# Gates taken straight from the adaLN sums, and a reordered pooling mixer

## The reference

```python
cond = jax.nn.silu(c)
for layer in range(2):
    mod = (cond @ ada_w[layer] + ada_b[layer]).reshape(B_, N_MOD, D)
    sh1, sc1, g1, sh2, sc2, g2, sh3, sc3, g3 = [mod[:, i] for i in range(N_MOD)]
    h = rmsnorm(x, norm_g[layer, 0]) * (1 + sc1) + sh1
    x = x + 0.5 * g1 * swiglu(h, ff_w13[layer, 0], ff_w2[layer, 0])
    h = rmsnorm(x, norm_g[layer, 1]) * (1 + sc2) + sh2
    mix = even_mixer(h, ...) if layer == 0 else multiscale_pool(h, pool_w[0], pool_b[0], pool_scale[0])
    x = x + g2 * mix
    h = rmsnorm(x, norm_g[layer, 2]) * (1 + sc3) + sh3
    x = x + 0.5 * g3 * swiglu(h, ff_w13[layer, 1], ff_w2[layer, 1])
# multiscale_pool: (((window mean of h) - h) @ w_grp, in 4 groups, + b_grp) * scale
# swiglu: (silu(a) * b) @ w2, with a, b = halves of h @ w13; width 2816
```

## Time and profile before

| | us |
|---|---|
| median of 3 runs (lowest, highest) | 1016.52 (1016.01, 1017.73) |
| the profiled execution, its own time | 1016.09 |
| its span, first to last instruction | 1014.0 |
| busy: TensorE, VectorE, ScalarE, GpSimd | 944.9, 727.4, 433.7, 102.7 |
| mean granted TensorE clock | 0.982 of 2.4 GHz |

### The profile page before, as it was taken

The page is one execution under the profiler, slowest core; times in us unless marked ns, Lnnn a source line. Parts: engine busy times, 40 slices in busy tenths (PEclk is TensorE's granted clock), DMA queues, the critical chain, the costliest instruction groups (busy, mean ns, idle before and its releaser), DMA issues.

```text
span 1014.0 us, 11292 instructions
## 1 busy us (share of the span) xinstructions
PE 944.9 (93%) x4368; PEld 772.7 (76%) x4368; DVE 727.4 (72%) x789; ACT 433.7 (43%) x555; POOL 102.7 (10%) x179
## 2 busy tenths in 40 slices
PE   4799999999889588999999999999999779999998
PEld 4688788887667457888888878888878668888886
DVE  4785978867778856879888677878775677654543
ACT  1444334344446554633333464333343464343431
POOL 2011111101402100011111000111110000000000
PEclk9999999999999789999999999999999979999999
DMA  9989998654994005999999459985894378656221
GB/s 341 376 291 376 377 318 272 228 179 147 327 231 134 34 20 180 351 319 325 349 313 338 170 163 324 298 293 188 290 305 161 103 228 303 206 166 208 83 79 47
DMA packets 147125, 239.34 MB, mean 236 GB/s; under 512 B 16128, under 2 KB 108160, under 8 KB 146944
## 3 DMA queue, kind: packets, MB, share of 16 engines
q1 hardware_dynamic: 126768, 167.01, 50.2%
q0 software_dynamic: 19440, 71.31, 20.1%
q10 hardware_dynamic: 864, 0.30, 0.1%
HBM read 237.54 MB, written 1.05 MB: 235 GB/s over the span
## 4 chain that ended last, share of the span: by engine, by line
PE 77%; DVE 8%; DMA 4%; ACT 4%; issue 3%; SPq 3%; POOL 1%; DVEq 0%; ACTq 0%
PE ps L1364 48%; PE ps L1421 7%; PE ps L1422 7%; PE ps L1425 7%; DMA raw<-in_ff_w 2%; SPq L389 2%; DMA raw<-in_w_in 2%; PE ps L1397 2%; DVE xn L983 1%; PE ps L1436 1%; PE ps L1456 1%; PE ps L1356 1%; DVE x L987 1%; ACT arena L601 1%; ACT hi L577 1%
## 5 line engine op out<-in xcount | busy, mean ns | idle before, releaser
L1364 PE MATMUL ps<-hi,hT_hi 128*128 128x512 f32 (+1 forms) x848 | 339.8, 401 | 13.6 <-DVE lo L874 6.1
L1364 PE MATMUL ps<-hi,hT_lo 128*128 128x512 f32 (+1 forms) x848 | 331.2, 391 | 0.0
L1364 PE MATMUL ps<-lo,hT_hi 128*128 128x512 f32 (+1 forms) x848 | 331.1, 390 | 0.0
L874 DVE TENSOR_TENSOR lo<-raw,hi 128x2048 fp32r<-128x2048 f32 (+1 forms) x76 | 171.6, 2261 | 44.2 <-ACT hi L577 44.1
L1364 PEld LDWEIGHTS ps<-hi,hT_hi 128*128 128x128 f32 x848 | 161.0, 190 | 52.3 <-issue 9.9
L1364 PEld LDWEIGHTS ps<-hi,hT_lo 128*128 128x128 f32 x848 | 160.8, 190 | 33.8
L1364 PEld LDWEIGHTS ps<-lo,hT_hi 128*128 128x128 f32 x848 | 161.2, 190 | 32.7 <-issue 1.4
L577 ACT ACTIVATE hi<-raw 128x2048 fp32r<-128x2048 f32 (+1 forms) x76 | 143.7, 1892 | 41.3 <-DMA raw<-in_ff_w 23.2
L480 POOL DMA_DIRECT2D ada<-in_ada_w x132 | 70.8, 537 | 503.7 <-DVE acc L926 193.4
L926 DVE SCALAR_TENSOR_TENSOR acc<-ada,cond,acc 128x1024 f32<-128x1024 f32 x73 | 93.6, 1282 | 10.5 <-DMA ada<-in_ada_w 6.9
L874 DVE TENSOR_TENSOR lo<-arena,hi 128x2048 fp32r<-128x2048 f32 x30 | 68.7, 2289 | 13.3 <-ACT hi L577 13.3
(11 more groups left out here) (162 smaller groups left out, 1071.9 us busy)
## 6 DMA issues: line engine op xcount, KB each, us to landing
raw<-in_ff_w SPq DMA_DIRECT2D x204, 512.0 KB, 5.6
ada<-in_ada_w POOLq DMA_DIRECT2D x132, 512.0 KB, 6.3
arena<-in_ff_w SPq DMA_DIRECT2D x60, 512.0 KB, 6.2
raw<-in_w_in SPq DMA_DIRECT2D x24, 512.0 KB, 7.6
arena<-in_ada_w SPq DMA_DIRECT2D x4, 1024.0 KB, 18.7
raw<-in_w_out SPq DMA_DIRECT2D x8, 512.0 KB, 4.6
raw<-in_ada_w SPq DMA_DIRECT2D x2, 1024.0 KB, 15.0
arena<-in_b_rpb SPq DMA_DIRECT2D x16, 128.0 KB, 9.9
```

The source lines that it names most:

```text
L874: ins = V.tensor_tensor(lo, src, hi.bitcast(F32), ALU.subtract)
L1364: ins = mm(out, a, b, start=first and m == 0, stop=last and m == len(pairs) - 1, skip_group_check=shared)
```

## The change

- The sum of a gate is not transposed any more. TensorE multiplies the adaLN buffer itself by ones, which sums over the partitions and spreads the result. The bias comes in at the start: ScalarE fills the buffer with eight diagonal blocks, `ident` times the bias column (`gate_start`), and VectorE's first tile adds to them in place of overwriting. The 0.5 is applied by ScalarE's copy.
- A gate is now made in the pair where its vector's sum would have been. `GATE_AT`, `diag`, `diag_buf` and `pool_gate` are gone.
- The vectors are worked on in the order `VECTORS`: 5 after 7, 11 after 13, 14 after 16. So the attention mixer's tiles are those of gate 5, and the last vector of feed-forward 2 is gate 14.
- Gate 14: VectorE multiplies its buffer by `pool_scale` at the end of feed-forward 2; TensorE makes the gate after `pool_average` of tile 0, ScalarE copies it ahead of `norm_out` of tile 1.
- ScalarE's and VectorE's splits of piece 84, and ScalarE's of 85, move into the end of feed-forward 2; VectorE's split of 85 stands ahead of the first difference.
- In the pooling mixer ScalarE takes norm and mean in twos; the biases of two groups are added together; tile 0's residual is done in both parts before tile 1's first, and tile 1's second before `norm_split` of tile 0. The squares follow that order.

The diff, cut to its core; for edits that only rename a wait's count "..." stands.

```diff
-GATE_AT = {(0, 8): 0, (1, 8): 2, (2, 7): 3, (2, 9): 4, (3, 9): 5}
+VECTORS = (0, 1, 2, 3, 4, 6, 7, 5, 8, 9, 10, 12, 13, 11, 15, 16, 14, 17)
...
+def is_gate(g):
+    return VECTORS[g] % 3 == 2
+def gate_of(g):
+    return VECTORS[g] // 3
+def columns_before(g):
+    return sum(not is_gate(i) for i in range(g))
+def acc_before(g):
+    return max(i for i in range(g) if (i in ACC_IN_XN) == (g in ACC_IN_XN))
+def first_pair(g):
+    return next((f, p) for f in range(4) for p in range(PAIRS) if (g, 0) in ada_in_pair(f, p))
...
 # scalar
             def gate_copy(k, half, bank):
                 act.wait_ge(gate_ps, 2 * k + half + 1)
-                dst = pool_gate if k == 4 else gate
-                nc.scalar.activation(dst[:, half * 512:half * 512 + 512], ps[:, bank, :], ACT.Copy).then_inc(gate_ready, 1)
+                nc.scalar.activation(gate[:, half * 512:half * 512 + 512], ps[:, bank, :], ACT.Copy,
+                                     scale=1.0 if k in (1, 4) else 0.5).then_inc(gate_ready, 1)
+            def gate_start(g):
+                before = acc_before(g)
+                if is_gate(before):
+                    act.wait_ge(gate_ps, 2 * gate_of(before) + 2)
+                else:
+                    act.wait_ge(mod_ps, 2 * columns_before(before) + 2)
+                if g == 13:
+                    act.wait_ge(xT_done, 16)
+                for k in range(KT):
+                    nc.scalar.activation(acc_of(g)[:, k * P:(k + 1) * P], ident[:, :], ACT.Copy,
+                                         scale=adab[:, VECTORS[g], k:k + 1]).then_inc(gate_bias, 1)
...
+                    for g in range(2, len(VECTORS)):
+                        if g != 7 and is_gate(g) and first_pair(g) == (f, p + 1):
+                            gate_start(g)
...
                 u_high_tile(f, 1)
+                if f == 2:
+                    split_hi(2 * FFN_PAIR[3])
                 if f < 3:
                     norm_out(s, 0, 4, 8)
+                if f == 2:
+                    split_hi(2 * FFN_PAIR[3] + 1)
...
             ffn(2)
+            for half in range(2):
+                gate_copy(4, half, half)
             g4 = NMOD + 3
-            for half in range(2):
-                norm_out(4, 1, 4 * half, 4 * half + 4)
-                for j in range(4 * half, 4 * half + 4):
+            for j2 in range(0, KT, 2):
+                norm_out(4, 1, j2, j2 + 2)
+                for j in range(j2, j2 + 2):
...
-            split_hi(2 * FFN_PAIR[3])
             norm_squares(5, 0, 0)
+            norm_squares(5, 0, 1)
             norm_squares(5, 1, 0)
-            norm_squares(5, 0, 1)
-            split_hi(2 * FFN_PAIR[3] + 1)
             norm_out(5, 0)
...
 # vector
                 if j == 0:
...
+                    if is_gate(g):
+                        dve.wait_ge(gate_bias, KT * (gate_of(g) + 1))
+                        V.scalar_tensor_tensor(dst, w, cond[:, 0:1], dst, ALU.mult, ALU.add).then_inc(ada_used, 1)
+                    else:
+                        V.tensor_scalar(dst, w, cond[:, 0:1], None, ALU.mult).then_inc(ada_used, 1)
...
                 u_low_tile(f, 1)
                 if f < 2:
                     norm_split(s, 0, ((4, 4),))
+                if f == 2:
+                    dve.wait_ge(pool_in, 32)
+                    dve.wait_ge(ada_used, ada_count(16, KT - 1))
+                    V.tensor_tensor(acc_of(16), acc_of(16), v_sb[:, 1, :], ALU.mult).then_inc(pool_step, 1)
+                    make_acol(5)
+                    split_lo(2 * FFN_PAIR[3])
                 residual(s, 1, y1_half, f + 1, part=0)
...
             ffn(2)
-            dve.wait_ge(pool_in, 32)
-            dve.wait_ge(gate_ready, 10)
-            V.tensor_tensor(gate[:, :], pool_gate, v_sb[:, 1, :], ALU.mult).then_inc(pool_step, 1)
+            split_lo(2 * FFN_PAIR[3] + 1)
...
-            dve.wait_ge(pool_step, 1)
-            make_acol(5)
-            split_lo(2 * FFN_PAIR[3])
-            for t in range(TT):
-                residual(5, t, unit_used, 2 * POOL_PAIR + 1, part=0)
+            residual(5, 0, unit_used, 2 * POOL_PAIR + 1, part=0)
             residual(5, 0, y0_done, 5, part=1)
+            residual(5, 1, unit_used, 2 * POOL_PAIR + 2, part=0)
             norm_scale(5, 0)
-            split_lo(2 * FFN_PAIR[3] + 1)
+            residual(5, 1, unit_used, 2 * POOL_PAIR + 2, part=1)
             norm_split(5, 0)
-            residual(5, 1, unit_used, 2 * POOL_PAIR + 2, part=1)
             norm_scale(5, 1)
...
 # tensor
-            def gate_half(k, half, bank, src=diag_buf):
-                pe.wait_ge(diag_done, KT * (k + 1))
-                mm(ps[:, bank, :], ones[:, :], src[:, half * 512:half * 512 + 512], start=True, stop=True
+            def gate_half(g, half, bank):
+                pe.wait_ge(ada_used, ada_count(g, KT - 1))
+                mm(ps[:, bank, :], ones[:, :], acc_of(g)[:, half * 512:half * 512 + 512], start=True, stop=True
                    ).then_inc(gate_ps, 1)
+            def sum_half(g, half, bank):
+                if half and is_gate(g):
+                    pe.wait_ge(gate_ready, 2 * gate_of(g) + 1)
+                elif half:
+                    pe.wait_ge(mod_red, 2 * columns_before(g) + 1)
+                (gate_half if is_gate(g) else mod_half)(g, half, bank)
+            def sum_read(g):
+                if is_gate(g):
+                    pe.wait_ge(gate_ready, 2 * gate_of(g) + 2)
+                else:
+                    pe.wait_ge(mod_red, 2 * columns_before(g) + 2)
...
+            def pool_bias(t, first=0, last=4):
+                for g in range(first, last):
+                    mm(ps[:, 2 * t + g // 2, (g % 2) * 256:(g % 2) * 256 + 256], ident[:, :],
+                       v_sb[:, 0, g * 256:(g + 1) * 256], start=g % 2 == 0, stop=False, skip_group_check=True)
...
             pool_average(0, 4, 8)
+            pe.wait_ge(h32_done, h32_count(4, 0, KT))
+            pe.wait_ge(pool_step, 1)
+            for half in range(2):
+                gate_half(16, half, half)
...
                 if g % 2 == 0:
                     pe.wait_ge(h32_done, h32_count(4, 1, 2 * g + 4))
-                for t in range(TT):
-                    mm(ps[:, 2 * t + g // 2, (g % 2) * 256:(g % 2) * 256 + 256], ident[:, :],
-                       v_sb[:, 0, g * 256:(g + 1) * 256], start=True, stop=False)
+                    for t in range(TT):
+                        pool_bias(t, g, g + 2)
```

More of the change, by code:

```diff
@@ L306, in build_program @@
         ada_used, mod_ps, mod_red, mod_done = sem("ada_used"), sem("mod_ps"), sem("mod_red"), sem("mod_done")
-        diag_done, gate_ps, gate_ready = sem("diag_done"), sem("gate_ps"), sem("gate_ready")
+        gate_bias, gate_ps, gate_ready = sem("gate_bias"), sem("gate_ps"), sem("gate_ready")
         x_tmp, x_done = sem("x_tmp"), sem("x_done")
@@ L647, in ffn @@
                 for p in range(LAST):
-                    gate_of = GATE_AT.get((f, p))
+                    g = sum_in_pair(f, p)
+                    gated = g is not None and is_gate(g)
                     if p:
@@ L915, in ada_tile @@
                 if j == 0:
-                    if g >= 2:
-                        before = max(h for h in range(g) if (h in ACC_IN_XN) == (g in ACC_IN_XN))
-                        dve.wait_ge(mod_ps, 2 * (before + 1))
-                    if g == 8:
-                        dve.wait_ge(gate_ps, 4)
-                    if g in (1, 9, 13):
-                        dve.wait_ge(xT_done, {1: 4, 9: 12, 13: 16}[g])
-                    V.tensor_scalar(dst, w, cond[:, 0:1], None, ALU.mult).then_inc(ada_used, 1)
+                    if g >= 2 and not is_gate(g):
+                        before = acc_before(g)
+                        if is_gate(before):
+                            dve.wait_ge(gate_ps, 2 * gate_of(before) + 2)
+                        else:
+                            dve.wait_ge(mod_ps, 2 * columns_before(before) + 2)
+                    if g in (1, 9):
+                        dve.wait_ge(xT_done, {1: 4, 9: 12}[g])
+                    if is_gate(g):
[3 more added lines that the diff above has]
+                        V.tensor_scalar(dst, w, cond[:, 0:1], None, ALU.mult).then_inc(ada_used, 1)
                 else:
@@ L1020, in ffn @@
                     tiles, g = ada_in_pair(f, p), sum_in_pair(f, p)
+                    if g is not None and is_gate(g):
+                        g = None
                     if p:
@@ L1464, in ffn @@
                 for p in range(1, LAST):
-                    g, k, spare = sum_in_pair(f, p), GATE_AT.get((f, p)), spare_bank(f, p) + 1
-                    summed = sum_in_pair(f, p - 1)
-                    if summed is not None:
-                        pe.wait_ge(mod_red, 2 * (summed + 1))
-                    if (f, p - 1) in GATE_AT:
-                        pe.wait_ge(gate_ready, 2 * GATE_AT[f, p - 1] + 2)
+                    g, spare = sum_in_pair(f, p), spare_bank(f, p) + 1
```

(13 more changed lines are left out.)

69 lines of the change are left out of this document (24 added, 45 removed).

## The result

| | before | after |
|---|---|---|
| median (lowest to highest), 4 runs each | 1017.12 (1016.01 to 1020.17) | 1007.29 (1002.47 to 1008.45) |
| the profiled execution | 1016.09 | 1008.45 |
| its span | 1014.0 | 1006.5 |

The account below looks back on a forecast made before the run. TensorE, busy 93% of the span, was taken as the bound. Terms 2.90 + 0.88 + 3.04 + 5.4 + 0.88 = 13.1 us off 1016.09 gave 1003.0, as a median 1003.4 us; 8 in 10 range 1000.3 to 1007.6.

Parts of the forecast that it names:

- Transposes of the gates: Six gate vectors no longer transposed; a vector's sum costs TensorE 0.88 us, a gate 1.72 us.
- the 1.72 of pair 8: Feed-forward 0: the gate moves from pair 8 to pair 3, so its 1.72 us at pair 8 go.
- Pair 3 of feed-forward 0: The gate's second half no longer waits for VectorE's reduction, so w2 begins 1.18 us earlier.
- Rival 3: Earlier gate doesn't help feed-forward 0, as the loads holding it up to 91 us return: 2.9 less, 1006.3; chance 0.08.
- Mixer: Attention mixer: 0 gained, bounds 0.53 us lost and 1.6 us gained or lost by the clock.
- Diagonals: Eight ScalarE bias instructions a gate at 0.30 us, 2.4 us (1.7 to 3.8), all hidden: 0; uncovered up to 3.8 us.
- End of feed-forward 2: Gate 11 and two sums replace four sums and two gates: 3.04 us, plus 0.44 counted in the tail; moved splits fit.
- what follows comes 0.44 us earlier (no half-sum): End of feed-forward 2: work after TensorE's w13 comes 0.44 us earlier, VectorE's tile 1 residual due at 789.33, not 789.77.
- Pooling mixer: Between feed-forwards 2 and 3: tile 1 starts at 821.35, not 826.76, at half clock: 5.4 us.
- rival 1: Pooling mixer: clock stays up through the shorter gap, 7.45 us gained there: 1001.4; chance 0.22.
- Rivals 2: Pooling mixer gives nothing, only matmuls count, 7.7 + 0.44: 1008.4; chance 0.12.
- 4 (late loads of 84 and 85): Slower: 84 and 85 landing late delay tile 1's squares and the pooling mixer: 1017 and more; chance 0.04.

Follow-up runs that it names:

- `before_a`: The kernel before, unchanged, run once more for the scatter of its own trace; 1019.56 us.
- `extra`: Changed kernel with four unread transposes put back ahead of every half of a gate, eight per gate vector; 1010.46 us, ratio 0.9911 to the kernel before.
- `swap23`: Changed kernel with vectors 2 and 3 swapped, so the sum is again in pair 3 of feed-forward 0; 1011.03 us, ratio 0.9926 to the kernel before.
- `order_old`: Changed kernel with tile 0's residual in one go undone and ScalarE's squares in their old order, splits left as changed; 1006.52 us.
- `clock_up`: Changed kernel plus 14 and 3 unused 512-column matmuls before and behind the pooling mixer's tile 0 transposes; 1004.68 us, ratio 0.9867 to the kernel before.
- `splits_back`: Changed kernel with only the splits of 84 and 85 back at their old places, residual in one go kept; 1011.08 us, ratio 0.9918 to the kernel before.
- `gates_only`: Changed kernel with the pooling mixer's splits, pooled pieces in fours, residuals' and squares' order put back; grouped biases and gate 14 stay; 1009.38 us.

## Why the prediction was right, and where it was off

The forecast was 1003.4, range 1000.3 to 1007.6; the median came to 1007.29, in the range, 3.9 over the forecast. It was right in sign and, in the main, in mechanism. The sum was too large in the terms that hang on waits, not in those made of matmuls. Between the two traces the gain is 7.5 of the 13.1 us forecast: 2.3 us are missing at the end of feed-forward 2 and in the pooling mixer, and the other 3.3 lie in ff0, the mixer and the first loads, which scatter. So the place inside the range, 0.3 us from its end, owes something to luck, and 7.5 us is itself one draw: the trace of `before_a` and the first of the changed kernel are 11.0 us apart.

- **Transposes of the gates.** The 0.88 of ff1 and ff3 measured 0.90 and 0.88, the 1.72 of pair 8 1.75. `extra` shows the cause.
- **Pair 3 of feed-forward 0, predicted 1.18.** From VectorE's split of the late weights to w2, the chain took 11.71 us before and 10.46 after: 1.25. Two things I had not in the term: the first matmul behind the remaining wait takes 0.27 us longer, and the loads came 0.6 to 1.2 us later, by scatter of their own (`before_a` has it too). Rival 3, "loads return", is what happened in part: ff0 gave 1.50 of 2.90 against the first trace of before (1.25 + 1.75 - 1.21 by the loads - 0.27). Against `before_a` it gave 3.7, for there the sum's wait cost the clock too. One trace of before could not show how far its own scatter reaches.
- **Mixer, predicted 0 with 1.6 us either way by the clock.** +0.84 between the two traces. Its loads scatter by 49.7 to 54.8 us and its rest by 105.3 to 107.0, with both traces of before at the low end. Four changed kernels are there too, at 105.3 to 105.5, so the change doesn't cost a fixed amount; whether it makes a slow rest likelier is open. The multiply-add does what was said: TensorE's wait near 258 us is 1.01 to 1.06 us in every changed kernel, 0.47 and 0.49 before, and it is swallowed by the loads.
- **Diagonals, estimated at 0.30 us each and hidden.** Eight take 2.44 us:

```profile
52.78 2.44 ACT L641 ACTIVATE acc<-ident,adab 128x128 f32<-128x128 f32 x8
```

  The estimate of 2.4 stands; the estimate of 3.2 from the budget in the Trainium skill ("ScalarE: Activation LUTs", Rules for kernel authors) is too high for these eight, issued back to back. Hidden they are, but by their place (`swap23`).
- **End of feed-forward 2, 3.04 and 0.44.** Measured 2.58 for both, from norm_scale to norm_scale; 2.5 to 2.9 in the other traces. The failed step is "what follows comes 0.44 us earlier (no half-sum)". w13 of tile 1 does end earlier, but the transposes behind it then wait for norm_scale, which ends at 778.63:

```profile
778.16 0.39 PE L1403 MATMUL ps<-hi,hT_lo 128*128 128x512 f32 x1
778.69 1.09 PE L1395 MATMUL ps<-ident,xn 128*128 128x128 f32 x8
```

  From w13's last matmul to these transposes it was 0.67 us with the half-sum between, and is 0.53 without it. Another 0.2 us is a wait for weights that were not in my list: the changed order lets GpSimd's loads for the pooling mixer go together with SyncE's, and one piece takes 12.88 us:

```profile
750.01 12.88 DMA raw<-in_pool_w
762.92 1.07 ACT hi L598
```

  TensorE waits 0.20 and 0.41 us for what follows from it in two traces, and under 0.1 in `order_old`, `clock_up` and `extra`. Together that is some 0.6 of the missing 0.9 us; the rest is not placed. Both splits, gate 14 and its copies fit where the prediction put them, for VectorE still idles ahead of tile 1's residual:

```profile
786.67 0.69 DVE L1027 TENSOR_TENSOR xn<-ps,gate 128x512 f32<-128x512 f32 x1 [0.72 <-PE ps L1446]
```

- **Pooling mixer, predicted 5.4, 4.97 of it behind norm_scale of the fourth norm.** Measured 3.58 there. By steps: the first difference gained 0.69 and not 0.93; to norm_scale of tile 0 2.49 and not 3.07, of which 0.34 is GpSimd's operation of 0.64 us in place of 0.30, begun while VectorE adds tile 1's residual; to the first w13 0.12 and not 0.43, to tile 1 0.28 and not 0.54. Half clock was the right choice, rival 1 the wrong one; `clock_up` prices the half clock at 2.2 to 3.3 us in the trace. The step that named the gain's origin was partly mistaken: I counted the split and tile 1's residual out of the stretch; `order_old` shows that the residual's place is worth nothing, and `splits_back` that the splits are worth all of it.

Rivals 2 (pooling gives nothing) and 4 (late loads of 84 and 85) fell.

## What to carry to other kernels

In a stretch where TensorE has no gap, an instruction taken out is worth its duration and can be booked as such; in a stretch that goes from engine to engine, book a moved operation only after walking the same chain to the next consumer, for the wait behind it takes its share: here the matmuls of feed-forwards 1 and 3 and of pair 8 paid 100%, those of feed-forward 2, whose end runs into norm_scale, 74% (2.58 of 3.48), steps of the pooling mixer 72% (3.58 of 4.97). A wait on TensorE costs its length and, where the clock falls, more behind it (1.5 us behind the 2.49 of `before_a`), so that a wait made short can be worth more than the chain says. And before a gain of a few microseconds is forecast from one trace, ask where that trace lies in the kernel's own scatter; a second trace of before told more here than most edits.

## What the runs showed of the hardware that I had not expected

- TensorE was at half clock behind waits of 2.49 and 3.13 us near 105 us and at full clock behind one of 2.18 in the same place. The wait's length alone does not decide: behind the 3.08 us before 795.15 in the kernel before, the granted clock stayed at 1.00. Behind 3.79 us at 808 us it fell; 17 unused matmuls in that gap and the next kept it at 1.00. The Trainium skill ("TensorE: Matmul & The Clock Gate", What's actually happening) says that the slow state is the default and that activity releases it; these traces agree, for after the gap of 3.79 us the clock came back while tile 0's matmuls ran, after eight of them in one trace and fourteen in another.
- A GpSimd operation on 128x1 took 0.30 us with VectorE idle and 0.64 to 0.72 us when it began while VectorE read two tiles of SBUF, in eight traces (the first of its two operations of this form 0.64, the second up to 0.72); moving VectorE's work away brought it back to 0.30 and 0.39. It seems to wait more than to run slower: each of them ended 0.17 us after VectorE's operation had.

```profile
806.23 0.69 DVE L1031 TENSOR_TENSOR x<-x,xn 128x512 f32<-128x512 f32 x1
806.45 0.64 POOL L512 TENSOR_SCALAR rstd<-ss 128x1 f32<-128x1 f32 x1 [15.23 <-ACT xn L610]
```

  The kernel before has it too: 1.02 us at 230.43, begun under a split of 2.29 us. Not every operation of VectorE does it: at 343.17 in the changed kernel one of GpSimd's on 128x8 took 0.20 us under one of VectorE's that reads a tile in PSUM and one in SBUF, and in `gates_only`, with VectorE idle, it took the same 0.20.
